# A second scan with narrower decay tables, its turns and value centring moved beside the projections, and one block for its output

## The chip, the cores and the metric

One Trainium2 chip, one of its cores. The metric is the device time of one execution in microseconds (us). Each kernel is run several times and the median counts. The engines are named as in the profile: PE (TensorE; PEld is its weight load), DVE (VectorE), ACT (ScalarE), POOL (GpSimd) and SP (the queue that starts most transfers).

## What is computed

A transformer block with three kinds of attention and a retrieved feed-forward layer, then two blocks of a second network: an mLSTM scan with 16 experts behind it, and a bidirectional retention scan with 16 experts behind it. All in float32, 256 tokens, width 1024. The change touches only the retention scan of the last block. What matters of the reference:

```python
def retention_scan(q, k, v, logg, S):       # per head; CHUNK = 64
    dmat = jnp.where(tril, jnp.exp(diff * logg[:, None, None]), 0.0)
    def step(S, inp):
        o = (q k^T * dmat) v + inter * (q S)
        S_new = sdec * S + (kdec k)^T v
# run_bidirectional: 256 context tokens first, then 256 latent tokens, forward;
# the same backward with its own decay; the two outputs of a latent token are added
def finish(y, g):
    mu = jnp.mean(y, axis=-1, keepdims=True)             # over the 128 of a head
    var = jnp.mean(jnp.square(y - mu), axis=-1, keepdims=True)
    y = ((y - mu) * lax.rsqrt(var + EPS)).reshape(b_, t_, h_ * d_) * gn_g
    y = y * jax.nn.silu(g)
    return y @ w_out
x = x + mod_l[2] * o_lat
x = x + mod_l[5] * expert_choice_ffn(...)               # 16 experts of 1024 x 1024 x 3
```

The kernel writes the scan out: for each head the weight of key token s for latent token t is q·k times a sum of two decay factors, exp(log g_forward x distance) and exp(log g_backward x distance), with a case distinction on the side of t on which s lies.

## The kernel before, in words

The program is a row of blocks; in each block every engine has its own list of instructions, and a block ends when all have ended. Order inside a block is written out by hand with semaphores. Weights come through a ring of six slots of 2 MB (`SLOTS`, `issue`): load n goes into the slot of load n-6 and is started by SP when that load has been used. SP's list is in order, so a load that waits holds back those behind it.

The last block of the network goes through `retention` (L2591) in this order:

- a norm and transpose (L326), which makes `ht`, 512 tokens (256 context, 256 latent) by 1024;
- **projections** in `gemm` (L391) with 28 tiles, L2639 to L2652: query 4 tiles, key 12, value 8, gate 4. PE's matmuls are recorded at L434, ACT moves each tile out of PSUM (L2651), and DVE applies the rotation to query and key beside it (`rope`, L2618). Four PSUM banks are used in turn;
- **turns**: two blocks of `turn` (L1128) put the latent keys and the queries of all heads with the head's 128 along the partitions. PE transposes at L1139, ACT copies at L1148;
- **heads** (L2668): POOL writes position numbers, DVE makes distances and masks of 1024 columns (4 key tiles of 256 latent tokens). For each of 8 heads ACT takes two exponentials of 1024 columns (L2697), DVE masks half of each (L2748), adds them (L2751) and multiplies them with the scores in PSUM (L2755); PE makes the scores of the next head (L2710) and the output of this one (L2722). ACT stores the output (L2682);
- **modulations** (class `Modulations`, L488): 24 products of a 2-row vector with 1024 x 512 weights, which other stages need. Each is 8 matmuls, recorded as 16, at L562, an ACT copy at L513, and 4 small turning matmuls at L546, which wait for that copy. Products 16 and 17 lie among the heads, 18 to 21 in `head_finish`, 22 and 23 in the norm of the expert stage;
- **finish** (`head_finish`, L2220): ACT takes Silu of the gate (L2232); DVE takes mean, subtracts, squares, sums, takes the inverse root, and multiplies with it and with the gate, each pass over 2048 columns (L2250 to L2259);
- a third `turn` (L1150), `row_gates` (L1946), which spreads a modulation over rows in PSUM by a diagonal matrix and a product with ones, and a **product with w_out** (`gated_out`, L2264), 4 tiles at L434, with a gated addition by DVE (L1983, L1984);
- `experts` (L2281): norm, router, gathering, then a loop over 16 experts with 6 loads of 2 MB each (L2454), matmuls at L2476. It is followed only by the final norm.

Of the kernel before, what the change touches and what calls it, by code (L numbers as in the profile page):

```python
# [17 lines left out]
I32 = mybir.dt.int32  # L18
# [5 lines left out]
P = 128  # L24
D = 1024
# [7 lines left out]
FIRST_MODS, BESIDE_UNITS, NEXT_MODS, BESIDE_HEADS, LAST_MODS = 4, 13, 16, 18, 22  # L33
# [357 lines left out]
def gemm(k, name, tiles, evac, upto, engine="act", banks=4, beside=None, between=None, behind=None,  # L391
# [29 lines left out]
    with nc.Block(no_gpsimd_drain=True) as block:  # L421
# [35 lines left out]
        if rows:  # L457
            @block.gpsimd
            def _(eng):
                k.expert_rows.pool(eng, rows)  # L460
                if pool:
                    pool(eng)
# [1483 lines left out]
def row_gates(k, name, layer, part, seqs, dst):  # L1946


    nc = k.nc
    diag = work(k, 20480, 256)  # L1950
    made, full, free = (k.shared[s] for s in ("diag_made", "row_full", "row_kept"))
    order = [(i, s, c) for i, s in enumerate(seqs) for c in range(C)]
    with nc.Block(no_gpsimd_drain=True) as block:
        @block.vector
        def _(dve):
            for j, (i, s, c) in enumerate(order):
                if j >= 2:
                    dve.wait_ge(*full.at(j - 1))
                dve.tensor_scalar(diag[:, P * (j % 2):P * (j % 2) + P], k.ident[:],
                                  k.mod[:, layer, part * C + c, s:s + 1], None, ALU.mult).then_inc(made.sem, 1)  # L1960

        @block.tensor
        def _(pe):
            for j, (i, s, c) in enumerate(order):
                pe.wait_ge(*made.at(j + 1))
                if j >= 4:
                    pe.wait_ge(*free.at(j - 3))
                pe.matmul(k.ps[:, j % 4, 0:P], k.ones[:], diag[:, P * (j % 2):P * (j % 2) + P],
                          start=True, stop=True).then_inc(full.sem, 1)

        @block.scalar
        def _(act):
            for j, (i, s, c) in enumerate(order):
                act.wait_ge(*full.at(j + 1))
                act.activation(dst[:, i, c * P:(c + 1) * P], k.ps[:, j % 4, 0:P], ACT.Copy).then_inc(free.sem, 1)
    for s in (made, full, free):
        s.base += len(order)


def add_gated(k, buf):  # L1980

    def evac(eng, t, ps):
        k.step_v.after(eng, eng.tensor_tensor(buf, ps, t.gate, ALU.mult))  # L1983
        return eng.tensor_tensor(t.dst, t.dst, buf, ALU.add)  # L1984
    return evac


# [230 lines left out]


def head_finish(k, name, y, tiles, heads, centre, gate, func, at, mods, span):  # L2220

    nc = k.nc
    n = tiles * heads
    sq = work(k, at, tiles * D)
    opened = k.sem(f"{name}_open")
    mean, ss, v, r, tmp = (k.small[:, 208 + 32 * j:208 + 32 * j + n] for j in range(5))
    y3 = y.rearrange("p a (h d) -> p (a h) d", d=P)
    s3 = sq.rearrange("p (n d) -> p n d", d=P)
    with nc.Block(no_gpsimd_drain=True) as block:
        @block.scalar  # L2230
        def _(act):
            act.activation(gate, gate, func).then_inc(opened, 1)  # L2232
            for a in range(*span):
                mods.scalar(act, a)

        @block.tensor
        def _(pe):
            for a in range(*span):
                mods.tensor(pe, a, a > span[0])
            mods.turn_rows(pe, span[1] - 1)  # L2240

        @block.sync
        def _(sp):
            issue(k, sp, k.numbers["ada"][span[1] - 1] + SLOTS + 1)

        @block.vector
        def _(dve):
            st = k.step_v.after
            if centre:
                st(dve, dve.tensor_reduce(mean, y3, AX.X, ALU.add))  # L2250
                st(dve, dve.tensor_scalar(mean, mean, 1.0 / P, None, ALU.mult))
                st(dve, dve.tensor_tensor(y3, y3, mean.unsqueeze(2).to_broadcast([P, n, P]), ALU.subtract))
            st(dve, dve.tensor_tensor(s3, y3, y3, ALU.mult))
            st(dve, dve.tensor_reduce(ss, s3, AX.X, ALU.add))
            st(dve, dve.tensor_scalar(v, ss, 1.0 / P, EPS, ALU.mult, ALU.add))
            rsqrt(k, dve, v, r, tmp)
            st(dve, dve.tensor_tensor(y3, y3, r.unsqueeze(2).to_broadcast([P, n, P]), ALU.mult))
            dve.wait_ge(opened, 1)
            st(dve, dve.tensor_tensor(y, y, gate, ALU.mult))  # L2259
            mods.vector_end(dve, *span)  # L2260
    retire(k)


def gated_out(k, name, y, tokens, col, stage, at, rows, layer, seqs):  # L2264

    yt = work(k, at, 4096)[:, 0:len(tokens) * D].rearrange("p (c t) -> p c t", c=C)
    gates = work(k, rows, len(seqs) * D).rearrange("p (s d) -> p s d", s=len(seqs))
    turn(k, f"{name}_y", y, yt, col)
    row_gates(k, f"{name}_rows", layer, 2, seqs, gates)
    n0 = k.stage[stage]  # L2270
    tiles = []
    for a in range(2):
        w = weights(k, n0 + a, 512)
# [617 lines left out]
```

## Time and profile before

| | us |
|---|---|
| median of 3 runs | 3035.7 (3030.65 to 3038.94) |
| profiled execution, device time | 3042.86 |
| its span on the engines | 3041.1 |
| granted TensorE clock, mean of the span | 0.871 |
| busy: PE / DVE / ACT / POOL | 2259.2 / 1329.7 / 458.3 / 810.4 |

The profile page cuts the span in 40 slices of 76 us. The retention stage is in slices 29 to 33, from 2180 us to 2491 us, where the transfers are mostly idle (page, second part: DMA tenths 2, 2, 2, 6). The slices behind it, the loop over the last experts, show the transfers at 9 tenths and 409 GB/s. The chain that the page follows back from the end covers only the final norm, so the argument uses the order of time.

### The profile page before, as it was taken

The page shows a single profiled execution, that of the slowest core. Times are in us where ns is not written, and L with a number is a line of the kernel's source. Part 1 is how long each engine was busy: PE and PEld are TensorE (multiplying, and loading weights), DVE is VectorE, ACT ScalarE, POOL GpSimd, SP SyncE. Part 2 cuts the span into 40 slices and gives each one's busy share as a digit, 9 for nine tenths or more (in the row PEclk, how much of TensorE's full clock was granted, in tenths as well). Part 3 has the DMA queues.
Part 4 walks back from the last instruction along what each step waited for, and adds up shares of the span by engine and source line. Part 5 has one row for each costly group of instructions (what it writes and reads, how often), then busy time and mean ns, then how long its engine had stood idle before and what let it go on. Part 6 is the DMA issues. An engine that isn't in the chain of part 4 may idle for free. (4 is left out here: it accounts for less than half of the span.)

```text
span 3041.1 us, 27001 instructions
## 1 busy us (share of the span) xinstructions
PE 2259.2 (74%) x9958; PEld 1104.3 (36%) x9958; DVE 1329.7 (44%) x2738; ACT 458.3 (15%) x905; POOL 810.4 (27%) x883
## 2 busy tenths in 40 slices
PE   7976797857747566559997998888699777555554
PEld 5544334624313222225654333222264534222222
DVE  3577344979986888754723011121210431101011
ACT  1322101212201111112223200000110412000000
POOL 2335433557777777740100000000000000000000
PEclk9986898978878778789997999999899987878887
DMA  9989999799999999995522699999822264999997
GB/s 372 390 282 352 383 380 329 290 357 393 380 339 370 373 375 379 372 336 183 199 106 112 272 406 410 410 410 410 335 83 94 100 222 175 409 409 409 410 410 286
DMA packets 294470, 966.19 MB, mean 318 GB/s; under 512 B 22369, under 2 KB 23521, under 8 KB 294241
## 3 DMA queue, kind: packets, MB, share of 16 engines
q1 hardware_dynamic: 182754, 562.20, 47.8%
q0 software_dynamic: 111616, 402.71, 35.5%
q8 instruction: 57, 0.93, 0.1%
q14 instruction: 43, 0.35, 0.0%
HBM read 896.67 MB, written 68.16 MB: 317 GB/s over the span
## 5 line engine op out<-in xcount | busy, mean ns | idle before, releaser
L2476 PE MATMUL ps<-big 128*32 128x256 f32 (+1 forms) x4608 | 589.2, 520 | 223.8 <-DMA big<-in_moe_w_up_dram 80.6
L434 PE MATMUL ps<-big 128*128 128x512 f32 (+3 forms) x1776 | 612.6, 506 | 24.3 <-PEq L332 7.9
L1839 PE MATMUL ps<-big 128*128 128x512 f32 x512 | 322.7, 771 | 221.2 <-ACT big L1857 148.6
L434 PEld LDWEIGHTS ps<-big 128*128 128x128 f32 (+1 forms) x1776 | 334.9, 192 | 293.9 <-issue 264.4
L2476 PEld LDWEIGHTS ps<-big 128*32 128x32 f32 (+1 forms) x4608 | 220.8, 136 | 574.0 <-issue 295.7
L1892 DVE SCALAR_TENSOR_TENSOR big<-big 128x1024 f32<-128x1024 f32 x256 | 313.8, 1227 | 106.2 <-DMA big<-peer_rows,big 102.4
L1790 POOL DMA_INDIRECT big<-in_peer_v_dram,big x256 | 305.7, 1194 | 110.7 <-issue 72.2
L1783 POOL DMA_INDIRECT big<-peer_rows,big x256 | 289.2, 1130 | 99.5 <-issue 76.2
L1839 PEld LDWEIGHTS ps<-big 128*128 128x128 f32 x512 | 113.7, 240 | 395.2 <-issue 215.2
L2576 DVE TENSOR_TENSOR big<-big,ps 128x512 f32<-128x512 f32 (+1 forms) x32 | 17.7, 554 | 500.7 <-issue 369.8
L605 POOL DMA_DIRECT2D peer_rows<-big x256 | 150.1, 593 | 312.4 <-DVE big L617 295.1
L2673 POOL IOTA big<- 128x1024 int32 x1 | 1.0, 992 | 853.1 <-POOLq L1132 853.1
L617 DVE STREAM_TRANSPOSE big<-big 128x1024 f32<-128x1024 f32 x128 | 151.0, 1221 | 131.9 <-DMA peer_rows<-big 119.2
L2559 DVE TENSOR_TENSOR big<-ps,big 32x256 f32<-32x256 f32 (+1 forms) x96 | 48.9, 510 | 293.7 <-PE ps L2476 291.7
L1879 DVE SCALAR_TENSOR_TENSOR big<-big 128x1024 f32<-128x1024 f32 x128 | 164.1, 1282 | 12.5 <-DMA big<-in_peer_v_dram,big 11.0
L2503 PE MATMUL ps<-big 128*128 128x512 f32 x160 | 83.1, 662 | 21.4 <-DVE big L2559 21.4
L1078 PE MATMUL ps<-big 128*128 128x512 f32 x192 | 88.4, 615 | 10.5 <-PEq L421 10.5
L1620 PE MATMUL ps<-big 128*128 128x512 f32 (+2 forms) x288 | 93.5, 479 | 0.0
L1428 PE MATMUL ps<-big 128*128 128x129 f32 x320 | 51.9, 318 | 46.4 <-DVE big L1466 46.4
L562 PE MATMUL ps<-big 128*2 128x512 f32 x384 | 58.7, 739 | 23.3 <-DMA big<-in_ada_w_dram 16.8
L2539 ACT ACTIVATE big<-ps 128x512 f32<-128x512 f32 (+1 forms) x32 | 15.7, 491 | 398.0 <-PE ps L2476 398.0
L2581 DVE TENSOR_TENSOR big<-big,ps 128x512 f32<-128x512 f32 x80 | 55.0, 687 | 39.2 <-PE ps L2503 39.2
(330 smaller groups left out, 2004.4 us busy)
## 6 DMA issues: line engine op xcount, KB each, us to landing
big<-in_moe_w_gate_dram SPq DMA_DIRECT2D x64, 2048.0 KB, 23.2
big<-in_moe_w_up_dram SPq DMA_DIRECT2D x64, 2048.0 KB, 23.5
big<-in_moe_w_down_dram SPq DMA_DIRECT2D x64, 2048.0 KB, 23.6
big<-in_peer_u_t_dram POOLq DMA_DIRECT2D x64, 1024.0 KB, 11.8
peer_rows<-big POOLq DMA_DIRECT2D x256, 256.0 KB, 6.9
big<-in_ada_w_dram SPq DMA_DIRECT2D x24, 2048.0 KB, 8.1
big<-in_mlstm_w_in_dram SPq DMA_DIRECT2D x12, 2048.0 KB, 18.0
big<-in_w_in_dram SPq DMA_DIRECT2D x8, 2048.0 KB, 19.2
```

The costliest lines, as they stand in the source:

```text
L434: last = pe.matmul(bank(i), lhsT, rhs, start=(j == 0), stop=(j == len(t.pairs) - 1))
L605: pool.dma_start(self.out[q][:, 8 * m:8 * m + 8], self.dst[m % self.OUT][32 * q:32 * q + 32] .rearrange("p j i c w -> p (j i) (c w)")).the ...
L617: dve.transpose(self.dst[m % self.OUT][:, j].rearrange("p i c w -> p c i w"), self.src[m % self.IN][:, j])\
L1078: pe.matmul(k.ps[:, i % 4, :], k.ht[:, c, t * P:(t + 1) * P], w[:, c, :], start=(c == 0), stop=False)
L1620: last = pe.matmul(self.bank(i), lhsT, rhs, start=(j == 0), stop=(j == len(t.pairs) - 1))
L1783: pool.indirect_dma_start(out=u_buf[n % NU], out_offset=None, in_=rows.rows, in_offset=bass.IndirectOffsetOnAxis(ap=index_of(0, n), axis=0))\
L1790: pool.indirect_dma_start(out=v_buf[n % NV], out_offset=None, in_=values, in_offset=bass.IndirectOffsetOnAxis(ap=index_of(1, n), axis=0))\
L1839: last = pe.matmul(k.ps[:, 4 + 2 * t + half, :], diag[n // 2 % 4], v_buf[n % NV][:, 512 * half:512 * half + 512], start=(n < PER and n % G ...
L1879: dve.scalar_tensor_tensor(out=x, in0=v_buf[n % NV], scalar=w[:, n:n + 1], in1=x, op0=ALU.mult, op1=ALU.add)\
L1892: dve.scalar_tensor_tensor(out=u, in0=u, scalar=1.0, in1=h2[:, t].rearrange("p q c w -> p (q c w)"), op0=ALU.mult, op1=ALU.mult, accum_out ...
L2476: last = pe.matmul(k.ps[q * M:q * M + M, bank, 0:W], lhsT(kc), w4[s][:, c, q * W:q * W + W], start=(kc == 0), stop=(kc == C - 1), skip_gro ...
L2503: pe.matmul(k.ps[:, 4 + j % 2, :], wb[:, t * P:(t + 1) * P], ys[:, 512 * nh:512 * nh + 512], start=True, stop=True).then_inc(c_full, 1)
```

## The change

It rewrites `retention` from the projections to the product with w_out:

- Decay tables. One table of 384 columns holds position differences from -128 on; each key tile reads its window of 256 columns from it. Per head ACT takes three exponentials of 384 columns (`scalar_exps`), DVE two operations of 384 columns on the argument (`vector_argument`), one addition and one multiplication of 384 columns (`vector_decay`), and the scores are multiplied in two halves of 512 columns. The tables of a head are made two heads ahead; those of heads 0 and 1, the logarithms and the position numbers are made beside the projections.
- Turns. The transposes of keys and queries are issued on PE behind projection tiles 18 to 25, two heads behind each, into PSUM banks 4 and 5.
- Values. DVE subtracts from the values their mean over each head while projections run, so the output of the scan has mean zero and the centring of the output goes.
- Gate. ACT moves the gate tiles out with Silu instead of Copy.
- Squares. ACT takes Square with a running sum from PSUM for each head and token tile, right behind the store; the inverse root is at the end of the block of heads.
- Modulations. Product 18 moves from the finish to the heads (`BESIDE_HEADS` 18 to 19).
- Out block. Row gates, products 19 to 21, scaling with the inverse root and gate, the third turn, and the product with w_out are one block without ends between them. Row gates are made with ACT's diagonals and one copy per 512 columns.

```diff
-FIRST_MODS, BESIDE_UNITS, NEXT_MODS, BESIDE_HEADS, LAST_MODS = 4, 13, 16, 18, 22
+FIRST_MODS, BESIDE_UNITS, NEXT_MODS, BESIDE_HEADS, LAST_MODS = 4, 13, 16, 19, 22
+    def vector_argument(dve, h):
+        e = decay[h % 4][:, 1, :]
+        k.step_v.after(dve, dve.tensor_scalar(e, place, minus[:, 8 + h:9 + h], None, ALU.mult))
+        dve.scalar_tensor_tensor(out=e, in0=place, scalar=logg[:, h:h + 1], in1=e, op0=ALU.mult,
+                                 op1=ALU.min).then_inc(argued, 1)
+    def scalar_exps(act, h):
+        act.wait_ge(argued, h + 1)
+        if h >= 2:
+            act.wait_ge(e_made, h - 1)
+        act.activation(e[:, 0, :], ahead_of, ACT.Exp, scale=logg[:, h:h + 1])
+        act.activation(other[...], behind_of[h >= 2], ACT.Exp, scale=logg[:, 8 + h:9 + h])
+        act.activation(e[:, 1, :], e[:, 1, :], ACT.Exp).then_inc(exped, 1)
+    def vector_decay(dve, h):
+        dve.wait_ge(exped, h + 1)
+        dve.tensor_tensor(e[:, 0, :], e[:, 0, :], other[...], ALU.add)
+        dve.tensor_tensor(e[:, 1, :], e[:, 1, :], twice, ALU.mult).then_inc(e_made, 1)
+    def turns(pe, i):
+        for n in turned_heads(i):              # i in 18..25, two heads each
+            pe.wait_ge(roped, 2)
+            if n >= 2:
+                pe.wait_ge(head_kept, n - 1)
+            for t in range(TT):
+                last = pe.transpose(k.ps[:, 4 + n % 2, t * P:t * P + P], src[:, t, h * P:(h + 1) * P], k.ident[:])
+            last.then_inc(head_turned, 1)
+    def centre_values(dve, stored):
+        for t in range(2 * TT):
+            stored(dve, value_tile[t])
+            st(dve, dve.tensor_reduce(mean, part, AX.X, ALU.add))
+            st(dve, dve.tensor_scalar(mean, mean, 1.0 / P, None, ALU.mult))
+            st(dve, dve.tensor_tensor(part, part, mean.unsqueeze(2).to_broadcast([P, B_HEADS, P]), ALU.subtract))
-    turn(k, "b_k", kk, kt_[:, :, T:2 * T], None)
-    turn(k, "b_q", q, qt, None)
         # heads, ACT
+            scalar_exps(act, 2)
+            for h in range(B_HEADS):
+                if h + 3 < B_HEADS:
+                    scalar_exps(act, h + 3)
                 act.wait_ge(o_full, h + 1)
+                act.activation(y[:, :, h * P:(h + 1) * P], out.rearrange("p (a d) -> p a d", a=2), ACT.Copy)
+                for t in range(TT):
+                    last = act.activation(square[t], out[:, t * P:t * P + P], ACT.Square,
+                                          accum_out=ss[:, TT * h + t:TT * h + t + 1])
+                last.then_inc(o_done, 1)
         # heads, DVE
+            st(dve, dve.tensor_scalar(behind_of[1], place, -1.0, float(T), ALU.mult, ALU.add))
+            vector_argument(dve, 2)
+            vector_argument(dve, 3)
             for h in range(B_HEADS):
+                dve.wait_ge(s_full, h + 1)
+                dve.wait_ge(e_made, h + 1)
+                for j in range(2):
+                    last = dve.scalar_tensor_tensor(out=wt[h % 2][...512 columns], in0=k.ps[...],
+                        scalar=B_DIM ** -0.5, in1=decay[h % 4][:, :, P * (1 - j):P * (1 - j) + T], ...)
+                last.then_inc(w_ready, 1)
+                if h + 2 < B_HEADS:
+                    vector_decay(dve, h + 2)
+                if h + 4 < B_HEADS:
+                    vector_argument(dve, h + 4)
+            dve.wait_ge(o_done, B_HEADS)
+            rsqrt(k, dve, var, r, tmp)
-    head_finish(k, "b_fin", y, 2, B_HEADS, True, gate, ACT.Silu, 4160, mods, (BESIDE_HEADS, LAST_MODS))
-    gated_out(k, "b", y, [k.x[:, 0, :], k.x[:, 1, :]], k.col("b_norm"), "b_out", 4160, 8256, 1, [0])
         # out block, PE
+            for c in range(C):
+                pe.wait_ge(diag_made, c + 1)
+                pe.matmul(k.ps[:, 4 + c // 4, P * (c % 4):P * (c % 4) + P], k.ones[:], diag[c % 4], ...)
+            for a in range(BESIDE_HEADS, LAST_MODS):
+                mods.tensor(pe, a, a > BESIDE_HEADS)
+            for h in range(B_HEADS):
+                pe.wait_ge(gated, h + 1)
+                ... two transposes
+            mods.turn_rows(pe, LAST_MODS - 1)
+            pe.wait_ge(kept, C)
+            pe.wait_ge(gate_kept, 2)
+            ... product with w_out, 4 tiles, banks 4 and 5
         # out block, DVE: 16 x (y * r * gate) of 128 columns, then the gated additions
         # out block, SP: issue(k, sp, k.stage["moe1"] + SLOTS - 2)
```

## Rows read from the trace of the kernel before

**Rows 1.** Busy time by stage: us, each engine busy (xinstructions), PEclk, DMA share, GB/s.

```profile
2199.70:2366.70 167.00, 166.89 (x448) 85.61 (x448) 17.64 (x29) 15.92 (x30) 0.00 (x0) 0.99 0.26 89
2366.70:2373.90 7.20, 4.30 (x32) 3.33 (x33) 0.00 (x0) 5.25 (x18) 0.02 (x1) 1.00 0.81 291
...
2550.00:3041.00 491.00, 275.85 (x3124) 121.85 (x3116) 54.66 (x129) 15.27 (x40) 0.00 (x0) 0.83 0.97 388
```

**Rows 2.** Order of time, last experts: start us, us, engine, work, [idle before, releaser].

```profile
2550.74 2.08 SPq L2454 DMA_DIRECT2D big<-in_moe_w_gate_dram  x2
...
2585.63 1.93 PE L2476 MATMUL ps<-big 128*32 128x256 f32 x32 [1.75 <-DMA big<-in_moe_w_down_dram]
```

**Rows 3.** Order of time, PE, from the last projections to the first scores.

```profile
2354.48 12.18 PE L434 MATMUL ps<-big 128*128 128x512 f32 x28
2367.66 2.15 PE L1139 MATMUL ps<-ident,big 128*128 128x128 f32 x16 [1.00 <-PEq L421]
...
2373.91 3.69 PE L2710 MATMUL ps<-big 128*128 128x256 f32 x16 [0.98 <-PEq L1132]
```

**Rows 4.** Order of time, PE, in the heads (L2722 output, L2710 scores, L546 turning).

```profile
2386.39 3.78 PE L2722 MATMUL ps<-big 128*128 128x128 f32 x16 [8.79 <-DVE big L2755]
...
2396.57 0.95 PE L546 MATMUL ps<-big 128*128 128x2 f32 x8
...
2399.28 1.99 PE L2710 MATMUL ps<-big 128*128 128x256 f32 x8
2401.11 1.95 PE L2722 MATMUL ps<-big 128*128 128x128 f32 x16
2402.89 1.89 PE L2710 MATMUL ps<-big 128*128 128x256 f32 x8
2406.11 2.05 PE L2722 MATMUL ps<-big 128*128 128x128 f32 x16 [1.33 <-DVE big L2755]
```

**Rows 5.** Groups by line and shape: work, count, busy us, mean ns, idle before.

```profile
L1983 DVE TENSOR_TENSOR big<-ps,big 128x512 f32<-128x512 f32 x4 | 2.8, 692 | 24.7 <-PE ps L434 24.7
...
L1000 DVE TENSOR_SCALAR big<-big,small 128x384 f32<-128x384 f32 x4 | 2.2, 548 | 0.1
...
L1434 ACT ACTIVATE big<-big 128x384 f32<-128x384 f32 x16 | 8.4, 523 | 212.1 <-DVE big L1456 212.1
...
L1012 ACT ACTIVATION_READ_ACCUMULATOR big<-big,small 128x1 f32 x16 | 3.0, 188 | 0.0
```

**Rows 6.** Order of time, DVE, in the finish, where the inverse root lies.

```profile
2440.60 0.17 DVE L2255 TENSOR_SCALAR small<-small 128x16 f32<-128x16 f32 x1
...
2443.11 2.29 DVE L2257 TENSOR_TENSOR big<-big,small 128x2048 f32<-128x2048 f32 x1
```

**Rows 7.** Order of time, PE, from the finish to the product with w_out.

```profile
2435.78 2.84 PE L562 MATMUL ps<-big 128*2 128x512 f32 x16
...
2441.11 3.59 PE L562 MATMUL ps<-big 128*2 128x512 f32 x16
2445.42 1.87 PE L546 MATMUL ps<-big 128*128 128x2 f32 x8 [0.72 <-ACT big L513]
...
2453.24 3.26 PE L1139 MATMUL ps<-ident,big 128*128 128x128 f32 x16 [0.86 <-PEq L2229]
...
2461.71 27.70 PE L434 MATMUL ps<-big 128*128 128x512 f32 x64 [0.68 <-PEq L1953]
```

**Rows 8.** Order of time, PE, in the norm of the experts.

```profile
2492.24 1.90 PE L562 MATMUL ps<-big 128*2 128x512 f32 x16 [2.83 <-PEq L1939]
...
2495.84 1.90 PE L562 MATMUL ps<-big 128*2 128x512 f32 x16
```

**Rows 9.** Order of time, ACT: a table load, the third turn's copies, a row gate's diagonals.

```profile
2377.41 1.28 ACT L2697 ACT_TABLE_LOAD   x1
...
2453.68 3.33 ACT L1150 ACTIVATE big<-ps,cols 128x256 f32<-128x256 f32 x8 [2.42 <-PE ps L1139]
...
2519.78 2.95 ACT L2359 ACTIVATE big<-ident,mod 128x128 f32<-128x128 f32 x8
```

More of the change, by code:

```diff
@@ L1943, in scaled_gains @@
     return gains_of(k, layer, part)
[L1946 to L1985, printed above, removed]
 def latent_scan(k, ctx_heads):
@@ L2217, in first_scan_out @@
     retire(k)
[L2220 to L2261, printed above, removed]
@@ L2264, in gated_out @@
[L2264 to L2273, printed above, removed]
-        cs = slice(512 * a, 512 * a + 512)
-        for j, x in enumerate(tokens):
-            tiles.append(tile([(yt[:, c, j * P:(j + 1) * P], w[:, c, :]) for c in range(C)], 512, n0 + a,
-                              dst=x[:, cs], gate=gates[:, j // TT, cs]))
-    gemm(k, f"{name}_out", tiles, add_gated(k, work(k, 19520, 512)), n0 + 2 + SLOTS, "dve")
@@ L2612, in retention @@
     mods = Modulations(k, 20992, NEXT_MODS, Modulations.TILES, (6,), k.ps[:, 7, 0:64])
[L2614 removed]
+    W = 3 * P
+    table = [work(k, 19776 + W * j, W) for j in range(3)]
+    place, twice, ahead_of = table
+    behind_of = [work(k, at, W) for at in (12352, 9792)]
+    numbers = work(k, 12352 + W, W).bitcast(I32)
+    decay = [k.big[:, at:at + 2 * W].rearrange("p (s c) -> p s c", s=2)
+             for at in (R_CTX, R_CTX + 2 * W, R_WORK + 8256, R_WORK + 8256 + 2 * W)]
@@ L2649, in retention @@
                 last_tile[a // 2, t - 2] = len(tiles)
-            tiles.append(tile([(ht[:, c, t * P:(t + 1) * P], w[:, c, :]) for c in range(C)], 512, n0 + a, dst=dst))
-    gemm(k, "b_in", tiles, lambda eng, t, ps: eng.activation(t.dst, ps, ACT.Copy), n0 + 8 + SLOTS, beside=rope,
-         between=modulation_start)
-    turn(k, "b_k", kk, kt_[:, :, T:2 * T], None)
-    qt = work(k, 18496, 2048).rearrange("p (h t) -> p h t", h=8)
-    turn(k, "b_q", q, qt, None)
-    dist = [work(k, 4160 + 1024 * j, 1024) for j in range(2)]
@@ new lines, in retention @@
+            tiles.append(tile([(ht[:, c, t * P:(t + 1) * P], w[:, c, :]) for c in range(C)], 512, n0 + a, dst=dst,
+                              gate=a >= 6))
+    gemm(k, "b_in", tiles, lambda eng, t, ps: eng.activation(t.dst, ps, ACT.Silu if t.gate else ACT.Copy), n0 + 8 + SLOTS,
+         beside=rope, between=scalar_beside, behind=turns, pool=numbered)
+    wt = [work(k, 4160 + 1024 * b, 1024) for b in range(2)]
+    w_ready, s_full, o_full, o_done, gated = (k.sem(f"ret_{s}") for s in ("weights", "scores", "out", "stored", "gated"))
```

213 lines of the change are left out of this document (152 added, 61 removed).

## The prediction, made before the changed kernel was run

> **What bounds the kernel now.** I read the busy time by stage first, then the order of time of PE through the retention stage, then DVE and ACT where PE waits. During the projections PE is busy 166.89 of 167.00 us at clock 0.99 [rows 1]. They are bound by PE, so whatever DVE and ACT do beside them is free while they keep up. The last stretch is bound by transfers: DMA share 0.97 at 388 GB/s, PE waiting for a weight transfer even late in an expert [rows 1, 2]. Its transfers start only when the first of the 16 experts has used a slot, at 2550.74 [rows 2]. Before that the ring is full, so nothing can be fetched earlier. A microsecond saved between the projections and 2550.74 therefore starts that stretch a microsecond earlier and ends the program a microsecond earlier. The question is only how long the way is from the last projection to the first product with w_out. PE ends the projections at 2366.66 (2354.48 + 12.18, [rows 3]) and starts the product at 2461.71 [rows 7]: 95.05 us. Nothing on it is bound by PE for long. The first output waits 8.79 us for tables and weights, and a head without a modulation goes from 2401.11 to 2406.11, 5.0 us, of which PE waits 1.33 for DVE [rows 4].
>
> **Beside the projections.** PE gains 32 transposes. Sixteen took 2.15 us [rows 3], so 4.3 us is added to PE, and it isn't hidden, since PE sets this stage. That is the one part that costs time. In exchange two blocks go, which held 7.25 us (2366.66 to 2373.91, [rows 3]), of which one change of blocks of 1.0 stays: net gain 7.25 - 1.0 - 4.3 = 1.95. PE's new waits: `roped` is two after tile 18. The last key tile is number 15; the rotation behind it is six passes over 512 columns at 0.692 [rows 5], 4.2 us, and tiles 16 to 18 take 3 x 6.9 (a quarter of the 27.70 that four tiles of the product with w_out took, [rows 7]; the projection tiles have the same shape). So 16 us of cover. `head_kept` waits for a copy of the tile before, a whole tile of cover. ACT: at tile 0 three table loads of 1.28 [rows 9] and small operations, some 4.7 against a tile of 6.9; at tile 6 one load and six exponentials of 384 columns at 0.523 [rows 5], 4.4 against four banks of slack, at least three tiles of 3.4. What queues behind these on ACT are the tiles' copies, and PE would feel it only beyond that. Each centring pass is 1024 columns, two passes of at most 1.4 (2 x 0.692), four times: 11 us of DVE with the last behind tile 23, and four gate tiles of 27 us to come. POOL, else idle here, makes 384 numbers. Each of these covers is over 10 us, so I cost them at nothing; where one fails, the excess is paid in full.
>
> The row on turns is the block after the projections, where the clock stayed at 1.00 through 32 transposes [rows 1], with the scores behind it at 1.9 a head [rows 3]. The Trainium skill, "TensorE: Matmul & The Clock Gate", Part 4, says that transposes don't count as a busy PE for the clock. By the row the sum keeps the 4.3; by the page the clock could fall in the gate tiles, which speaks against this change and is the third rival's reason.
>
> **Heads.** DVE begins with one operation on 384 columns and two arguments of two. No row has these exactly; the 384-column row with two operand columns is 0.548 [rows 5] and a plain 512-column pass 0.692, so 0.5 each, 2.6 in all (1.8 to 3.2). The scores of head 0 (half of 3.69, [rows 3]) are done by then. The multiplication is two halves at 0.692: first output at 2.6 + 1.4 + 0.2 = 4.2 after the block's first score, where before it was 12.5 (2373.91 to 2386.39). From there PE's own pitch counts: output 1.78 (2401.11 to 2402.89), scores 1.83 (2399.28 to 2401.11), turning and product of a modulation 2.71 (2396.57 to 2399.28) [rows 4]. So 8 x 1.78 + 6 x 1.83 + 3 x 2.71 = 33.4 and the last output ends at 4.2 + 33.4 + 0.2 = 37.8. Is PE the limit? DVE per head: 2 x 0.692 + 2 x 0.56 (384 columns, scaled down from 0.692) + 0.5 + 0.6 + gaps = 3.8 against PE's 3.6 without and 6.3 with a modulation; only head 3 has both no modulation and all of DVE's work, so it costs 0.2, within rounding. ACT: three exponentials 1.6, store 0.42 (3.33 for eight, [rows 9]), two squares at 0.28 (an estimate, two thirds of that copy for half the columns) with a reading of the sum of 0.188 each [rows 5], modulation 0.6: 3.6, under PE's 6.3. The two-heads lead means no exponential is waited for.
>
> The tail after the last output is new: store 0.42, squares 0.94, one operation and the inverse root 2.51 (2440.60 to 2443.11, [rows 6]), change of blocks 0.68 [rows 7]: 4.5. The out block starts at 37.8 + 4.5 = 42.3.
>
> **Out block.** ACT's eight diagonals, 2.95 [rows 9], PE's products one behind: 3.4. Three modulations: by the rows at full clock a pitch of 3.60 with a last product of 1.90 [rows 8]; at half clock 3.59 + 1.87 + 0.72 = 6.18; the one that began between is 5.33 (2435.78 to 2441.11) [rows 7]. Here PE comes from 4.5 us of idling and short diagonals, as it came from gaps in the finish before, so I take 5.33 twice and a last product of 3.59: 3.4 + 10.66 + 3.59 = 17.65. Then transposes 3.26 and the turning of product 21 at 1.87 [rows 7]: 22.8; ACT's copies (0.7 and 3.33) end at about 22 and are just hidden. All at full clock: 3.4 + 7.2 + 1.9 + 4.2 = 16.7. All at half: 24.5. DVE's 16 small passes, under 0.35 x 16 = 5.6, lie beside the modulations; that takes the old passes (mean, subtraction, squares, sums, about 9) off. In the old finish the modulations on PE (21 us at a pitch of 5.33, [rows 7]) were longer than those passes, so taking the passes off alone would bring little; what brings time is one modulation less, and row gates and scaling that lie beside it.
>
> SP: product 18's slot is free sooner and the loads behind it (22) earlier; 23 and the first four of the expert stage wait in the same order as before. None is needed within 30 us.
>
> **Sum.** New way: 4.3 + 1.0 + 42.3 + 22.8 = 70.4 against 95.05: 24.6 us less. The product itself, norm, router and first expert are as before. The profiled execution was 3042.86, 0.24% above the median of 3035.7; 3042.86 - 24.6 = 3018.3, a ratio of 0.9919, so by the median 3011.
>
> **Rivals.**
> - Full clock in the out block. For it: modulations right behind dense work ran at 1.90 [rows 8]. Against: the idle tail. 6.1 us less: 3005.
> - Square reloads the exponential's table. No row has Square on ACT. With Copy between exponentials there was one load for all heads (a single load at 2377.41, [rows 9]). If Square is not in that table, heads 0 to 4 pay 2 x 1.28 each: ACT 6.2 against PE's 6.3 in three of them, 5.5 against 3.6 in two, plus one load in the tail: 5 us back, 3016. The Trainium skill, "ScalarE: Activation LUTs", Table sets, names relu, copy, identity and abs as being in every set and not Square; it also gives a switch as about 2.66 us, where the row has 1.28.
> - Slower: the clock falls in the gate tiles. Transposes and their waits cut the dense stream eight times. A tile at half clock costs 6.9 more; from 24.6 / 6.9 = 3.6 such tiles on the gain is gone, and for all eight, +55 - 24.6: 3066. Against it: 0.54 us of transposes between 6.9 us of matmuls, and the clock of 1.00 through 32 in a row [rows 1]. This is the case that ends above 3036.
> - The covers beside the projections do not hold (rotation late, or ACT's tables late at tile 6), so that the change does not overlap what it says: 10 to 25 us come back, 3021 to 3036, about as before.
>
> **How the numbers follow.** Forecast 0.60, full clock 0.19, Square 0.09, covers fail 0.06, clock falls 0.06. About 0.3%, 9 us, is what a measurement of this kernel can tell from no change. Faster: forecast, full clock, Square and a third of the cover case, 0.89; same 0.06; slower 0.05. The range takes the full-clock case less what the tables may save (1 us) and run spread of 2 us: 3002. Above, it takes half clock throughout with a cold first output (3.78 for 2.05, [rows 4]) and a cold start of the product (3 us): +7 on 3011, and the Square case with part of it: 3021. Below 3002 I leave 0.05, above 3021 0.12.
>
> **What would show it.** In the profile after: projections 4.3 us longer at an unchanged clock; PE's first output about 4 us behind the first score; no PE wait for DVE over 0.3 us in heads 1 to 7 and a pitch of 3.6; one exponential table load in the heads and none between heads; 4 to 5 us of idle PE ahead of the out block; three modulations in it at a pitch over 5; 66 us from the end of the projections to the product. It is wrong if the loop over the last experts doesn't start earlier by the same amount, or its share of DMA changes.

## The result and the profile after

| | before | after |
|---|---|---|
| median (us) | 3033.18 (4 runs) | 3000.1 (4 runs) |
| profiled execution (us) | 3042.86 | 3007.82 |
| its span | 3041.1 | 3006.0 |

The table's median of before differs from the 3035.7 ahead of the prediction by one more run. The two medians are 33.1 us apart; the ratio is put at 0.9886, 95% interval 0.9870 to 0.9903, which is 34.6 us less (29 to 39), where 24.6 were forecast. The direction was right, but the time lies below the range (3002 to 3021).

Busy time by stage of the changed kernel (columns as in [rows 1]), the five stages from the projections to the last experts: projections, heads, out block up to the product with w_out, the product, the last experts.

```profile
2198.50:2368.90 170.40, 170.40 (x480) 88.78 (x480) 34.05 (x56) 28.83 (x58) 0.42 (x1) 0.99 0.25 87
2368.90:2411.50 42.60, 37.16 (x265) 30.30 (x264) 24.46 (x56) 19.94 (x65) 0.00 (x0) 1.00 0.56 198
2411.50:2427.83 16.33, 13.87 (x104) 8.96 (x105) 4.06 (x16) 8.29 (x20) 0.00 (x0) 0.90 0.61 224
2427.83:2455.60 27.77, 27.73 (x64) 12.10 (x64) 4.14 (x6) 0.00 (x0) 0.00 (x0) 1.00 0.45 171
...
2515.00:3006.00 491.00, 273.42 (x3128) 122.66 (x3120) 54.77 (x129) 15.25 (x40) 0.00 (x0) 0.81 0.97 388
```

The projections are still all PE, 3.5 us longer, at the same clock. The last 491 us have the same DMA share and rate as in [rows 1]. Their start is not put there by the choice of the window: the transfer for the last experts that [rows 2] has at 2550.74 begins 34.7 us earlier,

```profile
2516.06 2.09 SPq L2352 DMA_DIRECT2D big<-in_moe_w_gate_dram  x2
```

PE's order of time in the changed kernel, the counterpart of [rows 3], [rows 4] and [rows 7]:

```profile
2354.57 0.60 PE L2571 MATMUL ps<-ident,big 128*128 128x128 f32 x4
2355.01 13.90 PE L434 MATMUL ps<-big 128*128 128x512 f32 x32
2369.90 3.69 PE L2686 MATMUL ps<-big 128*128 128x256 f32 x16 [1.00 <-PEq L421]
2373.61 2.05 PE L2698 MATMUL ps<-big 128*128 128x128 f32 x16
...
2396.31 1.95 PE L2698 MATMUL ps<-big 128*128 128x128 f32 x16
...
2399.82 1.95 PE L2698 MATMUL ps<-big 128*128 128x128 f32 x16
...
2403.34 3.73 PE L2698 MATMUL ps<-big 128*128 128x128 f32 x32
2411.50 3.60 PE L2753 MATMUL ps<-big,ones 128*128 128x128 f32 x16 [4.43 <-ACT big L2783]
2415.03 1.90 PE L563 MATMUL ps<-big 128*2 128x512 f32 x16
2417.65 1.05 PE L547 MATMUL ps<-big 128*128 128x2 f32 x8 [0.72 <-ACT big L514]
2418.63 1.90 PE L563 MATMUL ps<-big 128*2 128x512 f32 x16
...
2427.83 27.73 PE L2773 MATMUL ps<-big 128*128 128x512 f32 x64 [1.02 <-ACT big L2792]
```

The projections end at 2368.91, and the first output starts 3.71 behind the first score, with no wait for DVE. Two outputs without a modulation are 3.51 apart (2396.31 to 2399.82). The last output ends at 2407.07; PE then has its one long gap, 4.43. The products of the out block come 3.60 apart (2415.03 to 2418.63), each in 1.90: full clock. (Of the two levels of TensorE's clock, the granted 1.00 is 2.4 GHz, full clock here, and 0.50 is 1.2 GHz, half clock; a value between is a stretch with both.) The row gates behind the gap take 3.60 at a granted clock of 0.54. From the end of the projections to the product it is 58.92 us, where it was 95.05 by [rows 3] and [rows 7].

I call this stretch **the way** from here on (end of the projections to the start of the product with w_out). In one execution it is read to 0.1 us. A second execution of the same kernel differed by 0.9 us for the changed kernel and by 3.8 for the kernel before (table below), while the times of a kernel vary by 8 to 20 us. So the way shows differences of a few us that the times can't, but not those below about 1 us, and beside the kernel before not those below about 4.

### The profile page after: what moved, and what is told of

It is laid out like the page before. It is cut to its first block and busy times, and to the rows that moved or that the text cites. A ratio compares the mean times of both kernels' runs of the same rounds, so it can differ in the third digit from the quotient of the medians.

```text
span 3006.0 us, 27016 instructions
## 1 busy us (share of the span) xinstructions
PE 2250.5 (75%) x9958; PEld 1102.7 (37%) x9958; DVE 1321.1 (44%) x2767; ACT 455.6 (15%) x945; POOL 805.9 (27%) x881
## 5 line engine op out<-in xcount | busy, mean ns | idle before, releaser
L434 PE MATMUL ps<-big 128*128 128x512 f32 (+3 forms) x1712 | 587.0, 503 | 22.8 <-PEq L332 7.4
L1840 PE MATMUL ps<-big 128*128 128x512 f32 x512 | 328.4, 784 | 220.4 <-ACT big L1858 157.7
L434 PEld LDWEIGHTS ps<-big 128*128 128x128 f32 (+1 forms) x1712 | 322.3, 192 | 274.0 <-issue 246.1
L1784 POOL DMA_INDIRECT big<-peer_rows,big x256 | 282.9, 1105 | 99.6 <-issue 76.2
L2401 PE MATMUL ps<-big 128*128 128x512 f32 x160 | 84.4, 671 | 21.4 <-DVE big L2457 21.4
L1079 PE MATMUL ps<-big 128*128 128x512 f32 x192 | 87.9, 612 | 11.1 <-PEq L421 11.1
L2479 DVE TENSOR_TENSOR big<-big,ps 128x512 f32<-128x512 f32 x80 | 55.0, 688 | 40.4 <-PE ps L2401 40.4
## 6 DMA issues: line engine op xcount, KB each, us to landing
big<-in_peer_u_t_dram POOLq DMA_DIRECT2D x64, 1024.0 KB, 11.6
```

Source lines behind the costliest of these rows:

```text
L434: last = pe.matmul(bank(i), lhsT, rhs, start=(j == 0), stop=(j == len(t.pairs) - 1))
L1079: pe.matmul(k.ps[:, i % 4, :], k.ht[:, c, t * P:(t + 1) * P], w[:, c, :], start=(c == 0), stop=False)
L1784: pool.indirect_dma_start(out=u_buf[n % NU], out_offset=None, in_=rows.rows, in_offset=bass.IndirectOffsetOnAxis(ap=index_of(0, n), axis=0))\
L1840: last = pe.matmul(k.ps[:, 4 + 2 * t + half, :], diag[n // 2 % 4], v_buf[n % NV][:, 512 * half:512 * half + 512], start=(n < PER and n % G ...
L2401: pe.matmul(k.ps[:, 4 + j % 2, :], wb[:, t * P:(t + 1) * P], ys[:, 512 * nh:512 * nh + 512], start=True, stop=True).then_inc(c_full, 1)
```

## The experiments

Times of different chips don't compare (the kernel before had a median of 3052 us on one and 3036 on another), so each is given as a ratio to the kernel before on its chip, beside the way.

| kernel | the way, us | product with w_out, us | ratio, 95% interval |
|---|---|---|---|
| before | 95.05 | 27.70 | |
| before_again | 91.24 | 30.01 | |
| before_no_silu | 91.82 | 30.08 | 0.9993 (0.9976 to 1.0010) |
| before_no_centre | 97.86 | 30.54 | 1.0003 (0.9988 to 1.0017) |
| before_narrow | 81.36 | 29.71 | 0.9950 (0.9932 to 0.9968) |
| the changed kernel | 58.92 | 27.73 | 0.9886 (0.9870 to 0.9903) |
| after_again | 59.81 | 27.73 | 0.9897 (0.9861 to 0.9934) |
| after_gap | 63.08 | 27.73 | 0.9889 (0.9851 to 0.9927) |
| after_turns_blocks | 66.43 | 27.73 | 0.9898 (0.9869 to 0.9927) |
| after_tables_late | 71.27 | 27.73 | 0.9927 (0.9903 to 0.9950) |
| after_out_split | 64.92 | 27.70 | 0.9904 (0.9880 to 0.9928) |
| after_no_lead | 59.01 | 27.73 | 0.9882 (0.9859 to 0.9906) |
| after_mods_in_tail | 54.39 | 27.73 | 0.9878 (0.9847 to 0.9910) |
| after_merged_tail | 52.62 | 27.73 | 0.9865 (0.9842 to 0.9887) |

The two theories at the start concern the step that failed, the pitch of the modulations. A: the order of work decides, that is, what stands on ACT between a product and its turning. B: it is the chance of an execution. (A modulation's product is copied by ACT, and PE then turns the copy with small matmuls, the turning.)

**The same kernels once more.** No edit.

> The changed kernel once more, for the place where the prediction failed: the three modulations of the out block, forecast at a pitch of 5.33 us and found at 3.60 with the clock at 1.00. Theory A (the order of work decides: here nothing on ACT stands between a product and its turning): pitch 3.60 again, 15 to 17 us from the out block's first product to the product with w_out. Theory B (chance of the execution): pitch somewhere from 3.6 to 6.1, the way up to 6 us longer. By both the time is 2997 to 3008.

> The kernel before once more. Its finish had four modulations at pitches of 4.69, 5.33 and 6.10 us with the clock falling to 0.5. Theory A: the same fall again, pitches over 5. Theory B: the fall may be absent, pitches of 3.6 to 4.7, and the way from the last projection to the product with w_out 88 to 92 us in place of 95.

PE of the changed kernel again, in the out block:

```profile
2425.65 2.58 PE L563 MATMUL ps<-big 128*2 128x512 f32 x16
2428.96 1.05 PE L547 MATMUL ps<-big 128*128 128x2 f32 x8 [0.73 <-ACT big L514]
2429.95 1.90 PE L563 MATMUL ps<-big 128*2 128x512 f32 x16
```

and PE of the kernel before again, in the finish:

```profile
2439.09 1.90 PE L562 MATMUL ps<-big 128*2 128x512 f32 x16 [0.78 <-PEq L2668]
2442.79 1.05 PE L546 MATMUL ps<-big 128*128 128x2 f32 x8 [1.80 <-ACT big L513]
2443.78 3.41 PE L562 MATMUL ps<-big 128*2 128x512 f32 x16
...
2448.87 1.90 PE L562 MATMUL ps<-big 128*2 128x512 f32 x16
```

Both theories have something. In the kernel before the second product is at half clock again (3.41), behind the 1.80 us wait for ACT, as A says. But here the clock is back for the third product (1.90), where in [rows 7] it was still down for the third (3.59), and in the same execution for the fourth too:

```profile
2447.21 3.38 PE L562 MATMUL ps<-big 128*2 128x512 f32 x16
```

So the length of the fall varies in one and the same kernel. The finish, up to the third turn, was 4.2 us shorter here; 2.3 of that came back in the product with w_out (30.01 instead of 27.70) and 1.4 in the row gates. In the changed kernel mainly the first product differs, 2.58 for 1.90, and the way is 0.9 longer.

**Taking the gap away, and putting it in.** `before_no_silu` leaves out the gate's Silu; `after_gap` adds one whose result nobody uses.

```diff
 # before_no_silu
-            act.activation(gate, gate, func).then_inc(opened, 1)
+            act.activation(gate[:, 0, 0:16], gate[:, 0, 0:16], ACT.Copy).then_inc(opened, 1)
 # after_gap, ACT ahead of the copies of products 19 to 21
+            spare = work(k, 4160, 2048)
+            act.activation(spare, spare, ACT.Silu)
```

> The kernel before with the Silu of the gate left out (16 columns copied in its place), so that ACT is free for the copy of product 18. The result is computed without the gate's Silu. Theory A (the 1.80 us wait of the first turning behind ACT's table load and Silu let PE idle, and the clock fell behind it): pitches of 3.6 at clock 1.00, the finish bound by DVE's passes, 17 us instead of 21, third turn 2.2 instead of 3.3; together 5 to 6 us less. Theory B (the clock falls because of the sparse work itself or by chance): only the 1.1 us of the longer wait go.

> The changed kernel with a useless Silu over 2048 columns on ACT ahead of the copy of product 19, as the kernel before had it. Theory A: 3.2 us of ACT's time (load 1.28, pass 1.91) open a gap of 2 to 3 us behind the first product, the clock falls to 0.5 afterwards, products 20 and 21 come at a pitch of 5.3 to 6.1, transposes take 3.3: 7 to 9 us more than the changed kernel. Theory B: only the gap itself, 2 to 3 us more.

Without the Silu, PE in the finish of the kernel before, up to the third turn:

```profile
2436.37 1.90 PE L562 MATMUL ps<-big 128*2 128x512 f32 x16 [0.78 <-PEq L2668]
...
2439.97 1.90 PE L562 MATMUL ps<-big 128*2 128x512 f32 x16
...
2453.80 3.65 PE L1139 MATMUL ps<-ident,big 128*128 128x128 f32 x16 [2.96 <-PEq L2229]
```

The four products come 3.60 apart, three times, as A expected. The 5 to 6 us that A expected of it did not come: the time is unchanged (0.9993), and the way, 91.82, is no shorter than the 91.24 of `before_again`. PE now ends the finish early and waits 2.96 for DVE's passes. The turn behind that wait (3.65), the row gates and the start of the product (30.08 in all, granted clock 0.50 in its first 3.9 us) come at half clock. Whether this is the fall of the finish, moved, is not shown: `before_again`, `before_narrow` and `before_no_centre`, with the Silu, had a slow turn and a slow start of the product as well.

With the Silu put into the changed kernel, PE in the out block:

```profile
2420.02 2.97 PE L563 MATMUL ps<-big 128*2 128x512 f32 x16
2424.97 1.28 PE L547 MATMUL ps<-big 128*128 128x2 f32 x8 [1.98 <-ACT big L514]
2426.18 3.30 PE L563 MATMUL ps<-big 128*2 128x512 f32 x16
...
2431.19 1.90 PE L563 MATMUL ps<-big 128*2 128x512 f32 x16
```

The pitches are 6.16 and 5.01 instead of 3.60. The way is 3.3 to 4.2 longer than in the two executions of the changed kernel, half of what A expected. Against the changed kernel 1.1 of the 4.2 is the first product, slow ahead of the Silu's gap (2.97, as in other executions without that gap), and 1.3 is the longer wait itself; the second product's half clock adds 1.4. So one product more is slow, not all that follow. The time does not show it (0.9889). Taken together, in all five profiled executions with the Silu ahead of the first copy the second product ran slow (2.84, 3.41, 3.20, 3.08 and 3.30 us), and in none of the seven that keep three or four modulations there without it (1.90 each). So in this place the gap decides whether the second product is slow; how long the fall lasts is not settled by it, and in another place of the same traces a second product is slow without such a wait (last section).

**Undoing the turns among the tiles.** `turned_heads` is left empty, and the two calls of `turn` stand behind the projections again.

> The changed kernel with the key and query turns back in two blocks between the projections and the heads. By the sum: the projections lose 3.5 us of transposes (measured in the changed kernel) and two blocks come, 6.25 us with their ends: 2.8 us more from the last projection's start to the product with w_out. If interleaving the turns had cost the projections anything beyond their own time, the difference is smaller or reversed.

The way is 66.43. Against the changed kernel's 58.92 plus the 3.5 us that its projections are longer, that is 4.0 more; 1.1 of it is a first product at 2.96 instead of 1.90. What is left, 2.9, is the forecast 2.8. Whether the turns cost the projections more than their own time has to be read from the projections, which the way leaves out. With the turns among them PE took 170.41 us in seven executions and 168.71 in one; without them 166.89 in three and 165.20 in three, this one too. Each has two levels 1.7 apart, and like levels differ by 3.5: the turns cost the projections their own time and nothing else.

**Undoing the early tables.** Logarithms, position numbers and the tables of heads 0 and 1 move to the start of the heads' block.

> The changed kernel with the logarithms, the position numbers and the tables of heads 0 and 1 in the block of heads. First output about 12.5 to 13 us behind the first score in place of 3.7, so 9 us more; behind it the clock may start at half for a first head (up to 3 us more). Rival: other work hides a part, below 6 us.

PE from the first scores on:

```profile
2359.39 3.69 PE L2682 MATMUL ps<-big 128*128 128x256 f32 x16 [0.99 <-PEq L421]
2371.72 3.78 PE L2694 MATMUL ps<-big 128*128 128x128 f32 x16 [8.64 <-DVE big L2723]
2375.43 2.66 PE L563 MATMUL ps<-big 128*2 128x512 f32 x16
```

The first output comes at 12.33, 8.6 later, and at half clock (3.78 and 2.66, 2.5 us more than 2.05 and 1.90); a first product of 2.95 in the out block adds 1.1. The way is 12.4 longer. The ratio rises to 0.9927. Of the parts undone singly this is the largest.

**Narrow tables alone, in the kernel before.** The other columns stay zero, so this kernel computes only part of the decays. Two passes that zero `wt` are not shown in the cut below.

```diff
 # before_narrow
-                        act.activation(ex[d], dist[d], ACT.Exp, ...
+                        act.activation(ex[d][:, 512:896], dist[d][:, 512:896], ACT.Exp, ...
-                    st(dve, dve.tensor_tensor(ex[j][:, 512:1024], ex[j][:, 512:1024], masks[j], ALU.mult))
+                    st(dve, dve.tensor_tensor(ex[j][:, 512:896], ex[j][:, 512:896], masks[j][:, 0:384], ALU.mult))
-                dve.tensor_tensor(wt[h % 2], ex[0], ex[1], ALU.add).then_inc(e_used, 1)
+                dve.tensor_tensor(wt[h % 2][:, 512:896], ex[0][:, 512:896], ex[1][:, 512:896], ALU.add).then_inc(e_used, 1)
```

> The kernel before with each pass on the decay tables cut from 1024 or 512 columns to 384 (exponentials, masks, sum), all else in its old order; the other columns of the tables are left zero, so only part of the decays is computed. Narrow tables alone: the heads without modulation go from 4.93 to 3.6 us a head (PE's own pitch), 5 to 6 heads: 7 us; the first output comes at 10 to 11 us instead of 12.5. Together 7 to 9 us under the kernel before. If the chain from ACT's exponential to DVE and back was the limit and not the width, the pitch stays over 4.3 and the gain is under 4.

PE in two heads without a modulation:

```profile
2402.19 1.95 PE L2722 MATMUL ps<-big 128*128 128x128 f32 x16
...
2405.70 1.95 PE L2722 MATMUL ps<-big 128*128 128x128 f32 x16
```

The pitch is 3.51, the wait for DVE of [rows 4] is gone, and the first output comes at 11.6 (2372.71 to 2384.30). From the first score to the end of the last output it is 45.0 us, where [rows 4]'s execution had 55.3: 10.3 less, a little over the 7 to 9 expected. Against `before_again` (54.8) it is 9.8. Of the 10.3, 1.7 is clock: the last output took 3.35 there behind a wait of 2.88 and 2.05 here behind one of 1.00, and the first product 2.92 and 2.57. The two zeroing passes, 0.91 each, end at 2381.21, where ACT's first exponentials were ready at 2380.10, so they cost about 1 us of the gain. The time falls by 0.50%, 15 us (10 to 21).

**The lead, and the centring.** In `after_no_lead` `vector_decay(dve, h)` stands ahead of the multiplication of the same head, for heads 2 to 7; in `before_no_centre` `head_finish` is called with its centring off, so the mean is left in the output.

> The changed kernel with DVE's addition and multiplication of a table right ahead of the scores' multiplication of the same head (heads 2 to 7), instead of two heads ahead. By the sum's reading DVE has idle time in every head but head 3, and PE is one head ahead with the scores, so at most 1 us more. If the lead is what keeps the heads at PE's pitch, 1 us in each of heads 2 to 7 is lost, 5 to 6 us more.

> The kernel before without the centring of the output in the finish (mean and subtraction left out, 4.75 us of DVE). The prediction said that this alone brings little, since the modulations on PE end the finish. From the last projection to the product with w_out: the kernel before had 95.05 and 91.2 us in two executions; here 90 to 95, the finish 17 to 21 us long and bound by PE. If DVE was the limit, up to 4.7 us less than that, under 88.

Without the lead the way is 59.01, between the changed kernel's two executions. DVE in head 4 (the first is head 0), in `after_no_lead`:

```profile
2386.44 0.55 DVE L2558 TENSOR_TENSOR big<-big 128x384 f32<-128x384 f32 x1
2386.91 0.55 DVE L2559 TENSOR_TENSOR big<-big 128x384 f32<-128x384 f32 x1
2390.45 1.29 DVE L2725 SCALAR_TENSOR_TENSOR big<-ps,big 128x512 f32<-128x512 f32 x2 [2.99 <-PE ps L2686]
```

The table is ready 3 us before the scores are, even when it is made last, and in heads 2 to 7 DVE still waits 1.1 to 3.0 for the scores. The lead of two heads costs and brings nothing measurable here. Without the centring DVE has 4.75 us less to do in the finish and nothing is gained: 1.0003, the way 97.86, the longest of all, because its modulations ran at half clock from the second to the last.

**The out block in four blocks.** Modulations beside the scaling, turn, row gates, product, each in a block, otherwise the changed kernel.

> The changed kernel with its out block cut into four blocks in the order of before: modulations beside DVE's scaling, turn, row gates, product. Order alone: modulations 1.9 + 2 x 3.6 + 1.8 = 11, turn 4, row gates 5.5, ends 3: 23 to 24 us against 16.8, so 7 more at full clock, and up to 12 more if the clock falls between. Theory A (merging is worth what it overlaps): 6 to 8. Theory B (its gain was mostly the clock): 2 to 3 at equal clocks.

The way is 64.92, 6.0 more. PE between the last output and the row gates:

```profile
2407.41 3.47 PE L563 MATMUL ps<-big 128*2 128x512 f32 x16 [4.00 <-PEq L2661]
...
2420.63 3.08 PE L1140 MATMUL ps<-ident,big 128*128 128x128 f32 x16 [0.80 <-PEq L2748]
2425.01 3.49 PE L2781 MATMUL ps<-big,ones 128*128 128x128 f32 x16 [1.30 <-ACT big L2789]
```

The first product took 3.47 and the turn 3.08, where the changed kernel had 1.90 and 1.97: 2.7 of the 6.0 are the clock, 3.3 the overlap. At equal clocks the value is thus nearer to theory B of this run (2 to 3) than to A (6 to 8). But the two can't be parted: in the changed kernel it is the row gates' short matmuls that stand behind the idle tail and take the half clock (3.60 at 0.54), and they wait for ACT's diagonals anyway.

**Filling the gap ahead of the out block.** PE's 4.43 us of idling and the 4.3 us of DVE's scaling suggested two versions. The first puts product 19 behind head 3 and products 20 and 21 behind the last output:

```diff
 # after_mods_in_tail, PE in the heads
-                if NEXT_MODS + h < BESIDE_HEADS:
+                if NEXT_MODS + h <= BESIDE_HEADS:
                     mods.tensor(pe, NEXT_MODS + h)
-                elif NEXT_MODS + h == BESIDE_HEADS:
-                    mods.turn_rows(pe, BESIDE_HEADS - 1)
+            for a in range(BESIDE_HEADS + 1, LAST_MODS):
+                mods.tensor(pe, a)
 # the same on ACT with mods.scalar; no modulations in the out block
```

> The changed kernel with product 19 behind head 3 and products 20 and 21 on PE right behind the last output, where PE is otherwise idle for 4.4 us while ACT and DVE make the inverse root. Product 19 costs the heads 2.7; the tail grows from 4.4 to about 5.5; the out block loses its three products, 9.2 us, and is then bound by DVE's 4.3 us and the turns: about 8 us. Together 3 to 5 us less than the changed kernel. Rival: the out block's short diagonals come at half clock and the wait for DVE takes the place of the products, 0 to 1 us.

The way is 54.39, 4.5 less, within the 3 to 5 expected. The second also moves the row gates (into banks 0 and 1, which the scores have left) and the scaling to the end of the heads' block:

> The version with modulations in the tail, and the row gates (into banks 0 and 1) and DVE's scaling moved into the tail too, so that the out block has only the turns and the product with w_out. Measured so far, from the start of the projections to the product with w_out: 229 to 230 us in the changed kernel, 224.8 with modulations in the tail. Here DVE's 4.3 us end the block of heads instead of PE's products; out block about 4 to 5 us ahead of the product: 222 to 224 us, 6 to 7 us under the changed kernel. Rival: the longer idle time of PE ahead of the turns halves the clock there and for the first product tile, 1 to 3 us back, no better than 224.8.

PE of `after_merged_tail` from the last output on:

```profile
2402.72 3.73 PE L2711 MATMUL ps<-big 128*128 128x128 f32 x32
...
2407.17 1.90 PE L563 MATMUL ps<-big 128*2 128x512 f32 x16
2409.00 2.35 PE L2720 MATMUL ps<-big,ones 128*128 128x128 f32 x16
...
2412.32 1.90 PE L563 MATMUL ps<-big 128*2 128x512 f32 x16
2415.24 1.94 PE L2776 MATMUL ps<-ident,big 128*128 128x128 f32 x16 [1.02 <-PEq L2664]
...
2418.98 27.73 PE L2788 MATMUL ps<-big 128*128 128x512 f32 x64 [1.01 <-ACT big L2797]
```

From the last output to the product no gap over 1.02 us is left, and the granted clock is 1.00 throughout. The way is 52.62, 6.3 less than the changed kernel's 58.92, and the ratio 0.9865. That lies below the changed kernel's 0.9886, but the intervals overlap: by one trace of it the way is about 6 us shorter, by the times alone a gain over the changed kernel is not shown.

## Why the prediction was right or wrong

Of the sum of 70.4, the changed kernel's trace shows 62.4 (58.92 + 3.5):

| term | forecast | measured |
|---|---|---|
| transposes in the projections | 4.3 | 3.5 |
| change of blocks | 1.0 | 1.0 |
| heads, to the end of the last output | 37.8 | 37.2 |
| (of it up to the first output) | (4.2) | (3.7) |
| tail of ACT and DVE | 4.5 | 4.0 |
| out block to the product | 22.8 | 16.8 |

(The out block is counted from 2411.05, where ACT makes its first diagonal.) The sum was 8.0 too high. The forecast of 3011 also started from a median of 3035.7, which one more run made 3033.2: 2.5 of the 10.9 us by which 3000.1 lies below it. The rest, 0.4, is within the spread.

**The failed step** is the size of the last term, the out block, and in it the pitch of the modulations. The prediction took 5.33 and 3.59 from the finish of the kernel before, and 3.26 for the transposes, as if an idle tail brought half clock to all that follows it. It had both levels in its rows and named full clock as a rival, at 0.19. In the changed kernel the pitch was 3.60, as in [rows 8], and the transposes took 1.97. The term came out 6.0 lower: 5.2 by the three products (9.0 where 14.25 were put), 1.5 by the transposes with their overlap, less 0.6 by the row gates, which took 4.0 for 3.4, and 0.1 by the last turning. What the prediction missed was in the same finish: the slow products came behind a first turning that waited for ACT, and ACT was busy with a table load and the gate's Silu. In the kernel before, ACT and then PE:

```profile
2432.34 1.91 ACT L2232 ACTIVATE big<-big 128x2048 f32<-128x2048 f32 x1
...
2434.79 1.05 PE L546 MATMUL ps<-big 128*128 128x2 f32 x8 [1.80 <-ACT big L513]
```

The change moves that Silu to the projections, where PE did not wait for it. `before_no_silu` and `after_gap` show that in this place this gap, and not the idle tail, is what made the second product slow. An idle tail of 4.43 us did halve the clock for the row gates (3.60 to 3.78) and, in some executions, for the first product (up to 2.97), and in the out block for nothing after it, in all five executions that have this gap there without the Silu. Why it stayed so short there no run explains.

**What the sum left out:** the product with w_out. The prediction took it as 27.70 on both sides, and put a cold start of it, 3 us, only into the upper end of the range. In the kernel before it took 29.7 to 30.5 in four of five executions of it and its variants, with a granted clock of 0.50 in its first 3 to 4 us; in the changed kernel and its variants 27.7 in all nine. In the profiled execution of before it happened to be 27.70, so this explains nothing of its 35.0 us, but it belongs to the difference of the medians.

**The rest.** 95.05 - 62.4 = 32.6 of the 35.0 us between the two profiled executions lie in the stretch. The projections started 1.3 earlier, where nothing was changed, and from the product's start to the end of the span it took 1.2 less. I count both as spread of executions. The ratio measured once more, 0.9897 or 31 us, fits.

**Right, as put:** the last experts' stretch started earlier by the same amount and kept its 0.97 share. The covers beside the projections all held (PE busy 170.40 of 170.40 us). The heads are at PE's own pitch (3.51). Early tables and narrow tables carry most (12.4 and 10.3 us where undone or done alone), turns 2.9, merging the out block 6.0, of which 2.7 were the clock. These were measured from different kernels and don't add up to the whole. Centring the values, the squares on ACT and the move of product 18 were not undone singly in the changed kernel, so their shares are open. That taking passes off DVE in the finish alone would bring little was right: `before_no_centre` brought nothing.

**The rivals.** Full clock in the out block came true: it put the block at 16.7, and 16.8 was measured. (The chances for faster add up to 0.90, not 0.89.) Square reloaded nothing: ACT in the heads, from a store on,

```profile
2388.25 0.21 ACT L2674 ACTIVATION_READ_ACCUMULATOR big<-ps 128x1 f32 x1
2390.21 0.60 ACT L514 ACTIVATE big<-ps 128x512 f32<-128x512 f32 x1 [1.75 <-PE ps L563]
2390.70 0.61 ACT L2551 ACTIVATE big<-big,small 128x384 f32<-128x384 f32 x1
```

goes from Square (L2674) to the exponential (L2551) with no load between, though the Trainium skill, "ScalarE: Activation LUTs", Table sets, does not name Square among the functions in every set. The clock did not fall in the gate tiles: the stage stayed at 0.99, and the transposes behind a tile took 0.44 (2354.57 to 2355.01). At 0.4 us per 6.9 the rule of the Trainium skill, "TensorE: Matmul & The Clock Gate", Part 4, that transposes don't count as a busy PE, made no difference. The kernel before speaks against it for these transposes: for 7.25 us (2366.66 to 2373.91, [rows 3]) PE did nothing but 32 of them, and the clock stayed at 1.00, where 4.43 us without work halved it. The claim that the two-heads lead matters was empty: `after_no_lead` is as fast.

Still open is why one fall of the clock lasts for one product and another for three, in the same kernel, and why an idle PE of about 3 us brings one in some executions and not in others.

## What to carry to other kernels

Before taking the half-clock durations of a stretch as the price of its successor, find the gap in front of them and ask whether the change keeps what made that gap; here a single ACT instruction and its table load, 3.2 us of ACT ahead of a product's copy, decided whether the next product was slow. Half-clock durations of sparse stages vary between executions of one kernel, so one profile is a weak source for them. Taking preparation out of a per-head loop paid most in its first head: 12.4 us for what was made beside an earlier stage bound by PE, while a lead inside the loop was worth nothing where DVE had 1 to 3 us to spare per head. An idle PE behind a loop can be filled with independent small products: in `after_merged_tail` its clock then stayed at 1.00.

## What the runs showed that I had not expected

- Slow clock can move instead of vanish. From the first product of the finish to the third turn it was 22.2 us in the kernel before, 17.4 in `before_no_silu` and 17.9 in `before_again`; from the third turn to the end of the product with w_out it was 36.2, 40.4 and 39.7. Most of what the first stretch gained the second lost. But that is no rule: in `before_no_centre` both were slow, 23.4 and 40.8. Of five executions the profiled one of before is the only one with a fast second stretch.
- It can also be hidden. In the norm of the experts the changed kernel's two modulations ran slow, and its router then waited less for its transfer. PE of the changed kernel there, to compare with [rows 8]:

```profile
2458.56 3.06 PE L563 MATMUL ps<-big 128*2 128x512 f32 x16 [2.99 <-PEq L1940]
...
2464.11 3.59 PE L563 MATMUL ps<-big 128*2 128x512 f32 x16
...
2477.15 7.01 PE L2227 MATMUL ps<-big 128*128 128x16 f32 x32 [3.35 <-DMA big<-in_moe_router_dram]
```

  In the execution of `after_again` both products took 1.90 and the wait for the router's transfer was 8.21. From the product with w_out to the gathering it was 68.92 us in the slow case and 67.89 in the fast one: of some 5 us of slow modulations 1.0 was left.
- An idle PE can bring half clock to two products in a row. In that same place, behind 2.83 to 3.00 us of idling and with only 0.7 us between a product and its turning, both products took 1.90 in nine of the fourteen profiled executions. In two the first was slow (3.39 and 3.50), and in three both were (3.06 and 3.59 in the changed kernel, 3.60 and 3.47 in `after_gap`, 2.99 and 3.59 in `after_no_lead`). So the prediction's idea that an idle tail slows all that follows did not hold in the out block, but it is not wrong everywhere, and the wait behind ACT is not the only way to a slow second product.
